# Two chained transformer blocks in float32 on one core: another order of the first heads' parts, more products on zeros

## The reference

```python
h = rms_norm(x, norm_mix_pre[l])
proj = h @ w_in[l]
qa, ka, va, qb, kb, vb = jnp.split(proj, SPLITS, axis=-1)
qa = apply_rope(rms_norm(qa.reshape(B, S, N_HEADS_A, HEAD_DIM), q_norm_a[l]), ang_axial)
ka = apply_rope(rms_norm(ka.reshape(B, S, N_KV_A, HEAD_DIM), k_norm_a[l]), ang_axial)
out_a = global_attention(qa, ka, va)
qb, kb = apply_rope(qb..., ang_1d), apply_rope(kb..., ang_1d)
out_b = window_attention(qb, kb, vb, sink_b[l])
mixed = jnp.concatenate([rms_norm(out_a, group_norm_a[l]),
                         rms_norm(out_b, group_norm_b[l])], axis=-1) @ w_out[l]
x = x + rms_norm(mixed, norm_mix_post[l])
f = (jax.nn.silu(h @ w_gate[l]) * (h @ w_up[l])) @ w_down[l]
```

## Time and profile before

| what | us |
|---|---|
| median of 3 runs | 1161.17 (1160.96 to 1161.55) |
| profiled execution, its own time | 1164.91 |
| its span, first to last instruction | 1163.1 |
| outside its span | 1.81 |
| PE busy in the span | 1133.3 |
| granted TensorE clock, mean | 0.995 |

### The profile page before, as it was taken

How to read it: one execution, slowest core, us unless ns; L and a number is a source line. 1 busy time by engine, 2 the same in 40 slices (tenths; PEclk the granted TensorE clock), 3 DMA queues, 4 the chain that set the end, 5 groups by cost and what they waited for, 6 DMA issues and landing times.

```text
span 1163.1 us, 15505 instructions
## 1 busy us (share of the span) xinstructions
PE 1133.3 (97%) x5560; PEld 936.3 (80%) x5560; DVE 650.2 (56%) x1085; ACT 503.0 (43%) x859; POOL 124.5 (11%) x143
## 2 busy tenths in 40 slices
PE   8999989999999999999999999999999999999997
PEld 6788767898888888888898887787888888888886
DVE  5888896966444444333378588563544444433333
ACT  5788885544223223222255458453322322332321
POOL 1476743000000000000000004200000000000000
PEclk8999999999999999999999999999999999999999
DMA  7321202213222222233223220032322222222312
GB/s 266 109 73 51 59 19 108 92 55 140 95 104 90 94 102 96 92 108 109 96 77 109 91 76 16 19 109 73 111 92 105 93 95 100 95 103 93 106 55 73
DMA packets 32515, 106.20 MB, mean 91 GB/s; under 512 B 4048, under 2 KB 6736, under 8 KB 32336
## 3 DMA queue, kind: packets, MB, share of 16 engines
q1 hardware_dynamic: 31712, 104.60, 25.5%
q10 hardware_dynamic: 752, 0.92, 0.3%
HBM read 100.78 MB, written 2.10 MB: 88 GB/s over the span
## 4 chain that ended last, share of the span: by engine, by line
PE 86%; DVE 6%; ACT 3%; POOL 2%; issue 2%; DMA 1%; ACTq 0%; SPq 0%; DVEq 0%; POOLq 0%
PE bank L502 24%; PE bank L504 24%; PE bank L503 23%; PE bank L1015 1%; PE bank L1005 1%; DVE wl L423 1%; PE bank L1088 1%; PE bank L963 1%; PE bank L964 1%; PE bank L965 1%; POOL pr L1335 1%; PE bank L1090 1%; PE bank L1089 1%; PE bank L2004 1%; PE bank L2002 1%
## 5 line engine op out<-in xcount | busy, mean ns | idle before, releaser
L423 DVE TENSOR_TENSOR wl<-raw,wh 128x1024 fp32r<-128x1024 f32 x181 | 223.9, 1238 | 299.3 <-ACT wh L415 299.2
L415 ACT ACTIVATE wh<-raw 128x1024 fp32r<-128x1024 f32 x181 | 191.1, 1057 | 420.3 <-PE bank L504 275.0
L502 PE MATMUL bank<-hh,wh 128*128 128x512 f32 x872 | 344.8, 395 | 4.3 <-DVE hl L1486 2.7
L504 PE MATMUL bank<-hh,wl 128*128 128x512 f32 x872 | 340.8, 391 | 0.0
L503 PE MATMUL bank<-hl,wh 128*128 128x512 f32 x872 | 340.6, 391 | 0.0
L502 PEld LDWEIGHTS bank<-hh,wh 128*128 128x128 f32 x872 | 164.4, 188 | 41.7 <-issue 4.8
L503 PEld LDWEIGHTS bank<-hl,wh 128*128 128x128 f32 x872 | 164.5, 189 | 35.3 <-issue 1.7
L504 PEld LDWEIGHTS bank<-hh,wl 128*128 128x128 f32 x872 | 164.2, 188 | 34.8
L504 PE MATMUL bank<-gh,wl 128*128 128x512 f32 x308 | 121.7, 395 | 0.0
L502 PE MATMUL bank<-gh,wh 128*128 128x512 f32 x308 | 121.7, 395 | 0.0
L503 PE MATMUL bank<-gl,wh 128*128 128x512 f32 x308 | 121.7, 395 | 0.0
(11 more groups left out here) (245 smaller groups left out, 1635.3 us busy)
## 6 DMA issues: line engine op xcount, KB each, us to landing
raw<-weights SPq DMA_DIRECT2D x181, 512.0 KB, 3.2
xres<-x_t SPq DMA_DIRECT2D x8, 512.0 KB, 7.6
sw<-ta SPq DMA_DIRECT2D x36, 64.0 KB, 2.0
out_t<-final SPq DMA_DIRECT2D x6, 256.0 KB, 2.5
rope<-angles SPq DMA_DIRECT2D x1, 1024.0 KB, 10.8
sw<-ta ACTq DMA_DIRECT2D x4, 64.0 KB, 3.1
wp<-pool_weights ACTq DMA_DIRECT2D x1, 256.0 KB, 2.6
out_t<-final ACTq DMA_DIRECT2D x1, 256.0 KB, 2.4
```

The costliest lines, as they stand in the source:

```text
L415: act.activation(wh[:, j, :, :], raw[:, j, :, :], ACT.Copy).then_inc(high_split, 1)
L423: v.tensor_tensor(wl[:, j, :, :], raw[:, j, :, :], wh[:, j, :, :].bitcast(F32), ALU.subtract)\
L502: pe.matmul(bank[:, :], wh[:, slot, b, :], ah[:, k, :], start=first and n == 0, stop=False)
L504: ins = pe.matmul(bank[:, :], wl[:, slot, b, :], ah[:, k, :], start=False, stop=last and n == len(blocks) - 1)
```

## The change

- `zeros(pe, n)` makes n products on the zero tile. `pe_start` makes 16 as before, then waits for the first `wh` chunk, makes 6 more, and `first_group` (new argument `idle`) makes 5 more ahead of its third piece, which is the first of tile 1.
- The parts of tiles 0 and 1 (k and q of head pair 0) are cut by head: `par` 0 in ticks -4 and -3, `par` 1 of k in ticks -2 and -1, `par` 1 of q in ticks 0 and 1. `KEYS` and `act_keys_low` work by head too, and `f1.keys` counts heads.
- `SPLIT_LOW` of 1 and 2 goes from ticks -1 and 1 to 1 and 2: DVE's cutting of chunks 5 and 6. ACT's (`SPLIT_AT`) stays in ticks -2 and 0.
- The sum of head squares of tile 3 ("pooled squares", `MIDDLE[3]`, tick 0) moves on PE behind the two pieces of that tick. `COS[3]` goes from tick -2 to 0, where POOL has nothing between.

```diff
-SPLIT_LOW.update({0: -5, 5: 14, 6: 16, 8: 29, 9: 37})
+SPLIT_LOW.update({0: -5, 1: 1, 2: 2, 5: 14, 6: 16, 8: 29, 9: 37})
...
-COS.update({0: -5, 1: -5})
+COS.update({0: -5, 1: -5, 3: 0})
...
-HIGH.update({(m, par): DONE[m] for m in EARLY1 for par in range(2)})
+HIGH.update({(0, 0): -4, (1, 0): -4, (0, 1): -2, (1, 1): 0})
...
-KEYS = {m: LOW[m, 1] + (0 if m in EARLY1 else 1) for m in ROPED if IN1[m][1] == "k"}
+KEYS = {(m, par): LOW[m, par] if m in EARLY1 else LOW[m, 1] + 1 for m in ROPED if IN1[m][1] == "k" for par in range(2)}
...
-        def first_group(pe, c0, t0, h, order):
+        def first_group(pe, c0, t0, h, order, idle=None):
...
-            for k, j in order:
+            for i, (k, j) in enumerate(order):
+                if i == idle:
+                    zeros(pe, 5)
...
+        def zeros(pe, n):
+            for _ in range(n):
+                pe.matmul(banks[7][:, :], cs[:, 0:P], cs[:, :], start=True, stop=True)
+
         def pe_start(pe):
             pe.wait_ge(cs_zeroed, 1)
-            for _ in range(16):
-                pe.matmul(banks[7][:, :], cs[:, 0:P], cs[:, :], start=True, stop=True)
+            zeros(pe, 16)
+            pe.wait_ge(high_split, 1)
+            zeros(pe, 6)
...
-            first_group(pe, 0, 0, h_in1, order)
+            first_group(pe, 0, 0, h_in1, order, 2)
...
-                if MIDDLE[m] == t:
+                if MIDDLE[m] == t and m != 3:
...
+            if t == MIDDLE[3]:
+                pe_middle1(pe, 3)
...
-                pe.wait_ge(f1.keys, kt + 1)
+                pe.wait_ge(f1.keys, 2 * kt + par + 1)
...
-        def act_keys_low(act, m):
+        def act_keys_low(act, m, par):
             i = IN1[m][2]
-            act.wait_ge(f1.part.low, parted(m))
-            for par, own, other in pair():
-                ins = act.activation(kl1[i][other, par, :], kl1[i][own, par, :].bitcast(F32), ACT.Copy)
-            ins.then_inc(f1.keys, 1)
+            _, own, other = list(pair())[par]
+            act.wait_ge(f1.part.low, parted(m, par))
+            act.activation(kl1[i][other, par, :], kl1[i][own, par, :].bitcast(F32), ACT.Copy).then_inc(f1.keys, 1)
```

More of the change, by code:

```diff
@@ L173 @@
 assert all(HIGH[m, 0] >= DONE[m] + 2 for m in LATER)
+assert [IN1[m][2] for m, par in KEYS] == [0, 0, 1, 1]
 assert all(COS[m] > LOW[ROPED[n], 1] for n, m in enumerate(ROPED[2:]))
@@ L191 @@
 WHOLE = {i: 4 * head_at(i, 1) + OUT_LAG + 1 for i in range(8)}
-assert all(LOW[tile1("q", HEADS1[s][1]), HEADS1[s][2]] < 4 * s and KEYS[tile1("k", HEADS1[s][3])] < 4 * s for s in range(len(HEADS1)))
+assert all(LOW[tile1("q", HEADS1[s][1]), HEADS1[s][2]] < 4 * s and KEYS[tile1("k", HEADS1[s][3]), HEADS1[s][2]] < 4 * s for s in range(len(HEADS1)))
 SUM_A = STEPS + TURN1 - 1
@@ L1269, in act_tick @@
                         act_part1(act, m, par)
-            for m in KEYS:
-                if t == KEYS[m]:
-                    act_keys_low(act, m)
+            for m, par in KEYS:
+                if t == KEYS[m, par]:
+                    act_keys_low(act, m, par)
             for m in NORMED:
```

## The result

| what | before | after |
|---|---|---|
| median of 8 runs, us | 1161.39 (1160.96 to 1161.88) | 1165.38 (1163.29 to 1167.01) |
| profiled execution, own time and span | 1164.91, 1163.1 | 1164.50, 1162.7 |
| mean granted clock in the profile | 0.995 | 0.997 |

The ratio is 1.0035, 95% interval 1.0026 to 1.0044: about 4 us slower, where 1160.2 and a range up to 1162.3 were forecast.

What follows compares the result with a forecast made beforehand. PE, busy 97% of the span, was taken to bound the kernel through its idle time and clock. 1161.17 less 1.8 for the clock at the start plus 0.85 for the later first turn gave 1160.2 us, range 1158.3 to 1162.3.

Steps and rivals of the forecast that it cites:

- I take 1.8 for the timed runs: Clock at the start, from 11.3 us: zeros keep it up, saving timed runs 1.8 us, between 1.4 and 2.7.
- rival 4: Zeros raise a clock that timed runs mostly had; only the 0.85 loss remains: 1161.5 to 1162, chance 0.12.
- Products on zeros cost nothing: Start of PE: six fill 1.4 of a 2.71 us wait for x, five take 1.15 before tile 1.
- the 23.4 forecast: With the clock up, PE reaches the sum of squares at 23.4 instead of 26.14 us.
- First scores 1.2 sooner, no wait, and the 0.5 gone: Parts by head: first scores start at 41.52, 1.2 us earlier, and the 0.5 wait for tile 3's squares goes.
- The whole 1.6 is given back in one wait of 2.1 us: Ahead of tile 5's first piece, PE waits 2.1 us for DVE's cut of chunk 5, losing its 1.6 lead.
- the chain to the cut: ACT and DVE steps from 39.70 to the cut of chunk 5, starting at 46.91 and ending at 48.68.
- Rival 3: The 2.1 us wait ahead of tile 5 makes the clock fall there: +1.5 us, 1161.7, chance 0.13.
- the condition that I set for it: Slow side above 1163.5 needs the first clock fall to cost its +0.5 bound too: +2.85, 1164.0, chance 0.03.
- The first turn 0.85 later: Cuts behind the maxima put the reciprocal at 55.10 and the first turn at 59.6 instead of 58.77: +0.85 us.
- The wait of 0.8 on POOL ahead of the turn: Ahead of the first turn PE waits 0.8 us on POOL's four products, where it waited 0.15 before.
- POOL's rotation of tile 3 starts later ... it costs nothing: Rotation starts 1.6 us later but ends before 53.5, ahead of the reciprocal at 55.1; tile 4's later swap costs nothing.

## Why the prediction was wrong

**The clock at the start: the step "I take 1.8 for the timed runs" failed.** The half clock of the earlier trace rows is real, and the zeros do keep PE busy there, but it is not the usual case. The sign was there: the profiled execution was 3.74 above the median, of which 1.81 lay outside its span. But 1161.2 is a span of 1159.4 with the same 1.8 outside it, so all 3.74 lay inside the profiled span: 2.7 is the half clock and 0.9 is x, which let PE's first piece start at 9.46 and not at 8.6 as in the changed kernel. The median timed run lost neither. I took the 1.81 for a part of the difference, when it is the same in both. The Trainium skill ("TensorE: Matmul & The Clock Gate", "What's actually happening") says that the point at which the clock changes is not tied to the kernel's start and varies from run to run. The two profiles of one program, with falls at 11.3 and at 42.4, agree. I had quoted it and then cut the 2.7 only to 1.8. With this term at nought the sum is 1162.0, my rival 4.

**Products on zeros cost nothing**: right in the median (1161.37 alone). The clock stays up at 11, the sum of squares stands at 22.68; 0.7 sooner than the 23.4 forecast because x arrived sooner in this execution.

**First scores 1.2 sooner, no wait, and the 0.5 gone**: right. Counted from the sum of squares they stood at 42.73 - 26.14 = 16.59, and stand at 38.06 - 22.68 = 15.38, which is 1.21 less.

**"The whole 1.6 is given back in one wait of 2.1 us"**: right in kind and place, too small in size. Two terms of the chain to the cut were mis-sized, both by POOL: the low part of q taken with 0.61 and measured 1.58 from start to start, and the cut taken with 1.77 and measured 2.18. The start of POOL's rotation was right: seen from the sum of squares it was to stand at 44.9 - 26.14 = 18.8 and stood at 41.40 - 22.68 = 18.7. But I let it begin to cover DVE only at 46.2, as if the gap behind its first product (2.45 in the old order, above) were still there. The swap had landed long before, its four products went end to end, and they met the low part of q already.

For the cut I took 1.77 from one row as what a cut costs beside POOL; the runs show 1.21 to 2.21. It depends on where in POOL's operation the cut begins. The Trainium skill ("SBUF — State Buffer", "SBUF: two separate sides") states a lock for the whole instruction. The runs agree: a cut can lose most of a POOL product's length (1.23 became 2.21), and a POOL product most of a cut's (1.28 became 2.27). Read that way the bound of the cut was 1.23 + 1.28 = 2.5, not 1.77.

**Rival 3, the new wait drops the clock, is half of what came**, given 0.13. The clock fell in a wait of 3.5, and filling the wait gives 2.0 of the 4.0 back; I had priced the fall at 1.5. The result stands above the 1163.5 that I had called slower without the condition that I set for it (a first fall that still costs), since the median timed run had nothing to win. The other 2.0 stays with the wait filled, since PE reaches tile 5 as late as in the change (46.87 and 46.76).

**The first turn 0.85 later**: it is 3.1 later. The profile to compare with is that of the zeros alone, where the clock stays up as well: sum of squares at 22.57 and first turn at 55.16, against 22.68 and 58.38, so 58.38 - 55.16 - 0.11 = 3.11. Against the forecast that is 2.2 more, and the reciprocal shows the same: forecast at 55.10, which is 51.64 on this axis (less 26.14 - 22.68 = 3.46), it stands at 53.86. Of that 1.5 is the later end of the cut. The other 0.7 lies behind it: the half clock lengthens six matmuls by 1.34, DVE waits 1.20 for the scores, and two cuts of 1.21 and 1.22, which I had counted with 1.68 from start to start, give part of it back. The wait of 0.8 on POOL ahead of the turn, which I had forecast, did not come, because PE itself was late.

**"POOL's rotation of tile 3 starts later ... it costs nothing"**: the step that failed for the parts by head. I asked whether the rotation would be done in time, and it was; I did not ask what stands beside it on DVE once its gap of 2.45 behind the first product is gone. Of the parts alone that costs 1.4 in cuts, and the two low parts moved from ahead of DVE's idle time to behind it cost 1.4 more, which is more than the 1.2 that the scores start sooner.

What stays open: why the parts add up to 3.4 and together cost 4.0, and why the whole change with both heads' k together costs only 0.8 over the kernel before when its part, only q by head, costs 1.7. Both differences are of the size of the intervals, and neither was taken apart.

## What to carry to other kernels

Before a profile's loss is taken as something to win, subtract what lies outside the span and see whether the timed runs have it; a profiled execution can be the unlucky one. Where VectorE works with two inputs from SBUF beside GpSimd, treat the two as one resource in time: here an operation moved out of a gap of the other engine cost up to its own length again, and moving it on only changed which operation it delayed. A wait that is freed at one place and comes back in one piece at a later one can cost more than it did: here two waits of 1.6 together became one of 3.5 with a fall of the clock in it.

## What the hardware showed that I had not expected

- The length of a wait does not tell whether the clock falls. Behind the wait of 2.09 PE worked at full speed from 46.03 to 47.3 before it went to half, and stayed there to 50.7; behind one of 1.89 at the same place it did not fall at all; but in the second profile of the kernel before it fell behind one of 1.59. In the wait of 3.54 it fell at 46.3, before PE went on. At the start of the kernel before, waits of 2.6 and 1.0 left it up in one profile, and those of 2.7 and 0.9 in the same stretch went with a fall at 11.3 in the other.
- Nine of the nineteen profiles have a half clock in a stretch between 148 and 158 us, where PE waits 1.2 and 0.8 on maxima. The other ten have the same waits there and no fall, and the versions differ only in their first 60 us. It is one reason why the profile of a version can't stand for its median: the parts by head alone have it (1164.23 against 1163.62), the later sum of squares alone has not.
- A GpSimd operation with one input from SBUF meets a cut as well. With one cut beside them the four products take 4.1 to 4.2, one of them about 1.7 where the shortest takes 0.69, and the cut takes 1.22 in some profiles and 1.66 in others; with two cuts beside them they take 5.2.
- In five versions, all with the added zeros, one to four of the 11 executions stand 1.2 to 2 us below all others: 1159.4 to 1160.0 against 1161.1 and more with the zeros alone, 1160.5 and 1160.6 against 1162.2 and more with chunks 6 and 7 late. The mean clock does not set them apart (0.998 in eight of the nine fast ones and in half or more of the others of each version). Whether the zeros do it, and how, stays open.
- Four transfers that ACT issues in a row (the swap of tile 1) are listed with 3.46 to 4.04 us on its queue in fifteen profiles and with 2.75 or 2.76 in four. This does not explain the groups: of the four, the change with its cuts back was its version's fastest execution (1161.42), but the one with chunk 7 late behind the early cut of chunk 5 was not (1163.20, where the fastest took 1160.70). First the zeros alone, then the change with its cuts back:

```profile
27.13 3.66 ACTq L1404 DMA_DIRECT2D sw<-ta  x4
```

```profile
27.03 2.76 ACTq L1406 DMA_DIRECT2D sw<-ta  x4
```
